# Routing by tiles, gathers and scatters that leave out empty places, results stored by token

## The reference

```python
def hier_moe(h, w_rg, w_re, w_g, w_u, w_d):
    T = h.shape[0]
    lg = (h @ w_rg).astype(jnp.float32)                 # 4 groups
    grp = jnp.argmax(lg, axis=-1)
    p_grp = jnp.take_along_axis(jax.nn.softmax(lg, axis=-1), grp[:, None], axis=-1)
    le = (h @ w_re).astype(jnp.float32).reshape(T, N_GROUPS, EXPERTS_PER_GROUP)
    le = jnp.take_along_axis(le, grp[:, None, None], axis=1)[:, 0]
    top_v, top_i = lax.top_k(le, TOP_K)                 # 2 experts of the group
    gates = p_grp * jax.nn.softmax(top_v, axis=-1)
    eid = (grp[:, None] * EXPERTS_PER_GROUP + top_i).astype(jnp.int32)
    return expert_dispatch(h, eid, gates.astype(h.dtype), w_g, w_u, w_d)
...
    # expert_dispatch, for each expert e and its tokens x:
    #   (silu(x @ w_g[e]) * (x @ w_u[e])) @ w_d[e], times the gate, summed by token
...
        x = x + mod[:, 5] * hier_moe(f_l, *moe_par).reshape(B, L, D)
```

## Time and profile before

| | |
|---|---|
| median of three runs | 2268.76 us |
| the profiled execution's own time | 2265.61 us |
| its span in the trace | 2263.5 us |
| PE busy | 1902.4 us (84%) |
| DVE busy | 814.9 us (36%) |
| ACT busy | 519.8 us (23%) |
| POOL busy | 82.5 us (4%) |
| moved by DMA | 376.37 MB |

### The profile page before, as it was taken

One profiled execution on the slowest core, in us unless ns is written; L12 is line 12 of the kernel. 1 busy time (PEld: TensorE's weight loads), 2 busy tenths in 40 slices (PEclk: granted clock), 3 DMA queues, 4 the chain that ended last, 5 costly groups with the idle time before them and its releaser, 6 DMA issues.

```text
span 2263.5 us, 29709 instructions
## 1 busy us (share of the span) xinstructions
PE 1902.4 (84%) x12822; PEld 1001.8 (44%) x12822; DVE 814.9 (36%) x1359; ACT 519.8 (23%) x957; POOL 82.5 (4%) x117
## 2 busy tenths in 40 slices
PE   5998569998998789978889889999974977777773
PEld 2443114643444555546666666664443332333231
DVE  2031533354645726434444544435335100000002
ACT  3001444321114512153233233113000000000001
POOL 0000000000000000020000000000000000000002
PEclk8999677599998899988899889999985999999997
DMA  8222343035111031031211111216415999999996
GB/s 338 75 74 75 112 159 139 27 137 218 59 37 38 0 135 47 0 127 43 67 49 54 62 43 49 90 35 270 159 64 224 416 428 426 426 427 426 428 427 242
DMA packets 49618, 376.37 MB, mean 166 GB/s; under 512 B 6033, under 2 KB 6177, under 8 KB 30795
## 3 DMA queue, kind: packets, MB, share of 16 engines
q1 hardware_dynamic: 36571, 317.85, 35.1%
q0 software_dynamic: 10032, 46.08, 5.6%
q10 hardware_dynamic: 2880, 10.49, 1.1%
HBM read 347.08 MB, written 31.51 MB: 167 GB/s over the span
## 4 chain that ended last, share of the span: by engine, by line
PE 40%; DMA 11%; DVE 8%; issue 2%; ACT 2%; POOL 0%; SPq 0%; DVEq 0%; ACTq 0%; POOLq 0%
PE psum L202 39%; DMA arena<-in_w 10%; DVE arena L149 4%; ACT arena L199 2%; DVE arena L159 1%; PE psum L205 1%; DVE arena L179 1%; DVE arena L167 1%; DVE arena L154 1%; DMA arena<-in_tok 0%; DVE arena L183 0%; DVE arena L187 0%; DVE arena L163 0%; DMA arena<-yd,arena 0%; DVE arena L175 0%
## 5 line engine op out<-in xcount | busy, mean ns | idle before, releaser
L202 PE MATMUL psum<-arena 64*64 64x32 f32 (+9 forms) x12174 | 1813.3, 372 | 303.0 <-ACT arena L199 104.2
L202 PEld LDWEIGHTS psum<-arena 64*64 64x64 f32 (+4 forms) x12174 | 922.5, 157 | 1135.3 <-issue 905.4
L199 ACT ACTIVATE arena<-psum 128x512 f32<-128x512 f32 (+6 forms) x389 | 206.5, 531 | 1195.9 <-PE psum L202 1083.2
L149 DVE TENSOR_TENSOR arena<-arena,psum 128x512 f32<-128x512 f32 (+1 forms) x136 | 75.5, 555 | 647.0 <-ACT arena L199 403.3
L199 ACT ACTIVATE arena<-arena 128x512 f32<-128x512 f32 (+10 forms) x242 | 135.4, 559 | 344.0 <-DVE arena L149 137.5
L149 DVE TENSOR_TENSOR arena<-arena 128x512 f32<-128x512 f32 (+11 forms) x312 | 195.4, 626 | 35.8 <-DMA arena<-in_norm_post 8.9
L149 DVE TENSOR_TENSOR arena<-psum,arena 128x256 f32<-128x256 f32 (+2 forms) x114 | 58.1, 509 | 253.8 <-PE psum L202 249.9
L159 DVE SCALAR_TENSOR_TENSOR arena<-arena 128x512 f32<-128x512 f32 (+5 forms) x138 | 111.4, 807 | 67.1 <-ACT arena L199 62.5
L205 PE MATMUL psum<-arena 128*128 128x128 f32 x648 | 108.3, 309 | 25.8 <-DVE arena L159 18.4
L205 PEld LDWEIGHTS psum<-arena 128*128 128x128 f32 x648 | 81.3, 157 | 93.3 <-issue 53.1
L199 ACT ACTIVATE arena<-psum,arena 128x128 f32<-128x128 f32 (+3 forms) x157 | 82.6, 526 | 173.0 <-PE psum L202 132.8
(11 more groups left out here) (46 smaller groups left out, 111.4 us busy)
## 6 DMA issues: line engine op xcount, KB each, us to landing
arena<-in_w SPq DMA_DIRECT2D x133, 2048.0 KB, 29.0
arena<-in_w SPq DMA_DIRECT2D x48, 256.0 KB, 3.0
yd<-arena ACTq DMA_DIRECT2D x16, 512.0 KB, 10.4
arena<-kd POOLq DMA_DIRECT2D x28, 256.0 KB, 3.9
gd<-arena SPq DMA_DIRECT2D x24, 256.0 KB, 3.1
arena<-gd SPq DMA_DIRECT2D x24, 256.0 KB, 8.4
yd<-in_zeros SPq DMA_DIRECT2D x1, 4096.0 KB, 18.6
arena<-in_w POOLq DMA_DIRECT2D x2, 2048.0 KB, 9.4
```

The source lines that it names most:

```text
L149: return self.ends(self.e.tensor_tensor(out, a, b, op))
L199: return self.ends(self.e.activation(out, a, func, **kw))
L202: return self.ends(self.e.matmul(out, lhs, rhs, start=start, stop=stop))
```

## The change

It does five things.

1. `gather` and `scatter` take `bounds_check=1023`, so a place whose index is over 1023 is left out. `IDX` now holds `NOBODY` = 2000 at empty places. POOL first fills the two `XG` buffers with zeros.
2. The result of a block no longer goes to `yd` by place from ACT, but is scattered by POOL to row `512 * j + token`, `j` being the first or second choice. For this `fd` is stored twice (rows 0 to 511 and 512 to 1023), so that one index serves for both. These stores move from ACT to POOL.
3. The tail reads `yd` in 8 plain loads of 128 rows from SP.
4. Ranks, places and the `slots` product are made tile by tile, woven between the output products; the order on PE, DVE and ACT changes with it, and ACT copies the turned tile ahead of the next tile's sum of squares.
5. What only the further blocks need (`EID`, their places and their `slots2` product) moves into the first 12 expert blocks, and the clearing of part of `yd` with zeros is gone.

```diff
     def gather(self, out, src, idx, signal):
-        self.e.indirect_dma_start(out, None, src, bass.IndirectOffsetOnAxis(ap=idx, axis=0)).then_inc(*signal)
+        self.e.indirect_dma_start(out, None, src, bass.IndirectOffsetOnAxis(ap=idx, axis=0), bounds_check=2 * S - 1, oob_is_err=False).then_inc(*signal)
...
     def scatter(self, dst, idx, src, signal):
-        self.e.indirect_dma_start(dst, bass.IndirectOffsetOnAxis(ap=idx, axis=0), src, None).then_inc(*signal)
+        self.e.indirect_dma_start(dst, bass.IndirectOffsetOnAxis(ap=idx, axis=0), src, None, bounds_check=2 * S - 1, oob_is_err=False).then_inc(*signal)
...
-    fd = internal("fd", (S, D))
-    yd = internal("yd", (128 * NB, D))
-    ydv = yd.rearrange("(r b) d -> r b d", b=NB)
+    fd = internal("fd", (2 * S, D))
+    yd = internal("yd", (2 * S, D))
+    ydv = yd.rearrange("(j t p) d -> j t p d", j=2, p=128)
...
-    fdv = fd.rearrange("(t p) d -> p t d", p=128)
+    fdv = fd.rearrange("(j t p) d -> j p t d", j=2, p=128)
...
+
...
+            def rank(i):
+                T.wait_ge(V["in", i], *ps.take(RANK, "rank", i))
+                T.mm(ps["rank", i][:, 0:32], C["tri"], IN[:, i, :], True, False)
+                T.mm(ps["rank", i][:, 0:32], ones, SUM[:, i, :], False, True).then_inc("rank", i)
+
+            def slots(i):
+                for j in range(2):
+                    T.wait_ge(V["slot", i, j])
+                    T.mm(ps["slots"][:, 0:NP], at_row(i, j), in_pair(i, j), (i, j) == (0, 0), (i, j) == (3, 1))
...
             for i in range(5):
                 if i < 4:
...
+                    out(i, 0)
+                if i > 1:
+                    rank(i - 2)
                 if i:
                     T.wait_ge(V["h3", i - 1])
...
+                    turn8("f4", i - 1, ht3[i - 1], SIX)
+                if i < 4:
+                    out(i, 1)
+                if i > 1:
+                    slots(i - 2)
+                if i:
+                    logits(i - 1)
+            rank(3)
+            slots(3)
             T.then_inc("slots")
+            T.wait_ge(*ps.take(RANK, "cnt"))
+            T.mm(ps["cnt"][:, 0:32], ones, SUM[:, 4, :], True, True).then_inc("cnt")
...
             for i in range(5):
+                if i:
+                    turn8_act("f4", i - 1, HT, i - 1)
                 if i < 4:
...
-                    A.wait_ge(V["h3", i])
-                    A.dma(fdv[:, i, :], ht3[i], d_fd.up(i))
-                if i:
-                    turn8_act("f4", i - 1, HT, i - 1)
...
+        def route_gpsimd():
+            G.wait_ge(T["ow", 0, 0], V["mg", 2, 7])
+            for b in XG:
+                G.zero(b)
+            G.mark("xg")
+            for i in range(4):
+                G.wait_ge(V["h3", i])
+                for j in range(2):
+                    G.dma(fdv[j, :, i, :], ht3[i], d_fd.up(j, i))
...
+                V.tt(SUM[:, i + 1, :], SUM[:, i, :], IN[:, i, :], ALU.add).then_inc("in", i)
+                V.ts(H64[:, i, :], EF[:, i, :], NP - 0.5, 64.0, ALU.is_ge, ALU.mult)
+                V.stt(COL[:, i, :], H64[:, i, :], -NP / 64.0, EF[:, i, :], ALU.mult, ALU.add)
+                for j in range(2):
+                    V.ts(in_pair(i, j), C["iota32"][:, 0:NP], COL[:, i, j:j + 1], TOKF[:, j, i:i + 1], ALU.is_equal, ALU.mult)
+
+            def place(i):
+
+                V.wait_ge(T["rank", i])
+                b, prod = ps["rank", i][:, 0:32], DM.rearrange("p (a j) e -> p a j e", a=2)[:, i % 2]
+                V.tt(prod, E12[:, i], bm(b, 2), ALU.mult)
+                V.red(R12[:, i, :].unsqueeze(2), prod, ALU.add)
+                V.ts(Q12[:, i, :], R12[:, i, :], 63.5, 1000.0, ALU.is_ge, ALU.mult)
+                V.tt(Q12[:, i, :], Q12[:, i, :], H64[:, i, :], ALU.add)
+                V.tt(P12[:, i, :], Q12[:, i, :], R12[:, i, :], ALU.add)
+                for j in range(2):
+                    V.ts(at_row(i, j), C["iota128"], P12[:, i, j:j + 1], None, ALU.is_equal).then_inc("slot", i, j)
+                V.cp(RK[:, i, :], b)
+                ps.free(V.last(), "rank", i)
 
...
+                    out(i, 0)
+                if i > 1:
+                    place(i - 2)
+                if i:
+                    turn8_dve("f4", i - 1, HT, i - 1)
+                if i < 4:
+                    out(i, 1)
                     V.then_inc("x2", i)
+                if i:
...
                 if i:
-                    route(i - 1)
-            V.then_inc("in")
...
+                    expert(i - 1)
+            place(3)
             V.wait_ge(T["slots"])
-            V.cp(IDX, ps["slots"][:, 0:NB]).then_inc("idx")
+            V.ts(IDX[:, 0:NP], ps["slots"][:, 0:NP], float(NOBODY), None, ALU.add).then_inc("idx")
             ps.free(V.last(), "slots")
-            V.cp(iovn, OVi[:, 31:32])
-            for j in range(2 * NO):
...
-            V.cp(iov, EID).then_inc("iov")
             V.ts(pg.unsqueeze(2), GM[:, :, 0:1], -1.0, None, ALU.mult)
...
+            V.wait_ge(T["cnt"])
+            V.cp(cnt, ps["cnt"][:, 0:32])
+            ps.free(V.last(), "cnt")
             V.mark("end5")
...
+        def over_slots_vector():
...
+            V.cp(iovn, OVi[:, 31:32])
+            for j in range(2 * NO):
+                V.ts(o1, OVi, j + 0.5, None, ALU.is_le)
+                V.red(EID[:, j:j + 1], o1, ALU.add)
+                if j % 4 == 3:
+                    yield
...
+            yield
+            V.wait_ge(T["slots2"])
+            V.ts(IDX[:, NP:NB], ps["slots2"][:, 0:NO], float(NOBODY), None, ALU.add)
...
         def experts_gpsimd():
-            G.wait_ge(V["idx"], d_fd[3])
-            for p in range(NP):
...
+            G.wait_ge(V["idx"], d_fd[1, 3], G["xg"])
+            for p in range(NP + 3):
+                if p < NP:
+                    if p > 1:
+                        G.wait_ge(T["tn", p - 2, 1])
+                    G.gather(XG[p % 2], fd, IDX[:, p:p + 1], d_xg[p % 2].up("xg", p))
+                if p > 2:
+                    G.wait_ge(A["yo", p - 3])
+                    G.scatter(yd, IDX[:, p - 3:p - 2], YO[(p - 3) % 2], d_yo[(p - 3) % 2].up("yo", p - 3))
+                if p == NP - 1:
+                    G.wait_ge(T["slots2"])
                     G.dma(rowC, mods2[0, 5120:6144].partition_broadcast(128), d_rc.up("rowC"))
...
+                over_slots(p)
...
+                if p:
+                    next(over_slots, None)
...
-                    A.wait_ge(A.last())
-                    A.dma(ydv[:, first + p - 1, :], YO[(p - 1) % 2], yo[(p - 1) % 2].up("yo", p - 1))
+                    A.mark("yo", p - 1)
...
         def tail_gpsimd():
-            tG.wait_ge(*end6(), d_y0["y0"])
-            for i in range(4):
-                for j in range(2):
-                    tG.gather(y12[i][j], yd, DI[:, i, j:j + 1], d_y12[i].up(j))
             for i in (0, 2):
...
         def tail_sync():
+            Y.wait_ge(*end6())
+            for i in range(4):
+                for j in range(2):
+                    Y.dma(y12[i][j], ydv[j, i], d_y12[i].up(j))
             for i in range(4):
                 Y.wait_ge(tV["x3", i] if i % 2 else tG["x3", i])
```

More of the change, by code:

```diff
@@ L27 @@
 WOVEN = 14
-SMALL = 1972
+SMALL = 1864
+NOBODY = 2000
 COL_SPEC = [
@@ L2116, in route_tensor, with out, logits @@
         def route_tensor():
-            T.wait_ge(V["mg", 2, 7])
+            def out(i, hf):
+                T.wait_ge(W.landed(43 + hf), *ps.take(SIX, "ow", i, hf))
+                for k in range(8):
+                    T.mm(ps["ow", i, hf], MG[:, k, c4(i)], wk(43 + hf)[:, k, :], k == 0, k == 7)
+                T.then_inc("ow", i, hf)
+                if i == 3:
+                    T.mark("w", 43 + hf)
+            def logits(i):
+                T.wait_ge(A["f4", i, 0], V["f4", i, 1], d_rt["wr"], *ps.take(SIX, "rt", i))
+                for k in range(8):
+                    T.mm(ps["rt", i][:, 0:36], HT[:, k, c4(i)], WRT[:, k, :], k == 0, k == 7)
+                T.then_inc("rt", i)
@@ new lines, in rank @@
+            def rank(i):
[6 more added lines that the diff above has]
+                    T.mm(ps["slots"][:, 0:NP], at_row(i, j), in_pair(i, j), (i, j) == (0, 0), (i, j) == (3, 1))
+            T.wait_ge(V["mg", 2, 7], *ps.take(SLOT, "slots"))
@@ L2162, in route_scalar, with out, group @@
             A.mark("end5")
+        def route_gpsimd():
[7 more added lines that the diff above has]
+                    G.dma(fdv[j, :, i, :], ht3[i], d_fd.up(j, i))
         def route_vector():
             ss = small
-            def route(i):
-                turn8_dve("f4", i, HT, i)
+            def out(i, hf):
+                xs = X[:, i, hf * 512:(hf + 1) * 512]
+                V.wait_ge(T["ow", i, hf])
+                V.tt(tt_[hf], ps["ow", i, hf], rowA[:, hf * 512:(hf + 1) * 512], ALU.mult)
+                ps.free(V.last(), "ow", i, hf)
+                V.wait_ge(d_xb["x"])
+                V.tt(xs, xs, tt_[hf], ALU.add)
+            def group(i):
                 V.wait_ge(T["rt", i])
```

(19 more changed lines are left out.)

171 lines of the change are left out of this document (83 added, 88 removed).

## The result

The changed kernel takes 2228.24 us (2227.04 to 2229.0, 4 runs) and the kernel before 2268.62 (2266.03 to 2268.77, 4 runs, three of them those of the table ahead of the prediction): ratio 0.9824, interval 0.9807 to 0.9841, faster by 40.4 us. The forecast was 2225.3, 43.5 less. The profiled execution took 2227.04 with a span of 2225.2, which is 38.3 under the span of before. They fall 5.2 us short of the forecast's 43.5, where the medians fall 3.1 short: the profiled execution of before was 3.0 under its median, and that of after 1.2.

The account below looks back on a forecast made before the run. Expert blocks were held bound by DMA, mostly weights, their start by routing; gains of 18.9 + 12.8 + 1.3 + 9.0 + 1.5 = 43.5 us took the median from 2268.76 to 2225.3, range 2212 to 2239.

Parts of the forecast that it names:

- likeliest case: Whole kernel: the forecast itself, its own terms leaving it at 2220 to 2231 us; chance 51%.
- Routing's tiles: From the end of `ow(1,1)` to that of `ow(3,1)`: 54.3 us become 35.4 without PE's pauses, gain 18.9 us.
- Routing's end: From `ow(3,1)` to the table: 37.7 us become 24.9, including 1.1 for hand-overs, gain 12.8 us.
- Table to block 0: From the table to block 0's first product: 12.2 us become 10.9 with a gather of 8.0, gain 1.3 us.
- EID: Ahead of block 0: moving it frees DVE when the turned tile comes, which takes out 2.8 us.
- Rows left out: Expert blocks' gathers and scatters: skipping empty places gains 9.0 us, taken between 0 and 18.1.
- third possibility: Expert blocks: DMA engines have fixed places and the fullest sets the end, gaining less than the mean, down to 0.
- rows shared evenly: Expert blocks: the heaviest DMA engine gains as much as the mean, 18.1 us for 9.0, giving 2216; chance 17%.
- empty places cost like full ones: Expert blocks: a descriptor is still made and moved for each, gain 0 for 9.0, giving 2234; chance 20%.
- slower rival: Expert blocks: transfers with rows left out run on fewer DMA engines; 2270.6 us with filled rows on four; chance 4%.
- Tail: After ACT's last copy: scatter loses 2.6 us, plain reads give 3 to 4 back; gain 1.5, between -2 and 4.
- The new order waits: Routing's tiles: `rank(i)` waits for DVE, PE pauses and a tile takes 22 us for 17.2, giving 2238; chance 8%.

Follow-up runs that it names:

- e7: The kernel before, with only ACT's copy of the turned tile moved ahead of the next tile's sum of squares and store: 2263.81 us, ratio 0.9991.
- e3: The changed kernel with empty places moved as full rows, reading a row of zeros and writing an unused row: 2236.98 us, ratio 0.9865 to the kernel before.
- e2: The changed kernel with an expert's first eight tokens in rows 0 to 3 and 32 to 35: 2235.61 us, ratio 0.9861 to the kernel before.
- e4: The changed kernel with the last two of eight weight loads held until block 0's gather landed: 2217.87 us, ratio 0.9790 to the kernel before.
- e5: The changed kernel with EID's 32 DVE operations back between index table and gates: 2227.27 us, ratio 0.9815 to the kernel before.
- e9: The changed kernel with two weight loads held for the first gather and EID back ahead of the gates: 2225.22 us, ratio 0.9813 to the kernel before.
- e10: The changed kernel run again unaltered, as base for its neighbours: 2226.62 us, ratio 0.9821 to the kernel before; first expert product to last 32 products 470.0 us.
- e1: The changed kernel with an expert's places dealt round, its first eight tokens in rows 0, 4, 8 to 28: 2222.35 us, ratio 0.9804 to the kernel before.

## Why the prediction was right, and where it was off

The result lies 2.9 us above the forecast and inside the likeliest case's own range, 2220 to 2231. By the two profiles the gain is 5.2 under the forecast: 1.9 of that is the later start, which no step foresaw and which lies within scatter. By its steps:

- **Routing's tiles: right.** 18.8 for 18.9, PE full at 1.00 as foretold. But the cause was half told. The prediction named ACT's copy alone; e7 shows that DVE's stood as far behind and that freeing one alone brings nothing that can be told. The sum came out since the change moves both.
- **Routing's end: 14.8 for 12.8.** Counted from the end of `ow(3,1)`, `rank(2)` was forecast at 8.5 us and came at 8.3, the last logits at 12.5 and 12.3, `rank(3)` at 19.4 and 19.1, the table at 23.8 and 22.9. The 1.1 us for hand-overs on top was wrong: durations read from the timeline held them already.
- **Table to block 0: the failed step.** It reads "With under half of the rows of block 0 filled I take 8.0, between the two." The gather took 10.6, and POOL issued it 0.9 after the table, which the sum left out: 2.6 and 0.9 account for the 3.4 us between +1.3 and -2.1. (Before, POOL issued it 0.3 after the table; why it is 0.9 now isn't shown.) Fewer rows hardly shorten a gather that lies behind weight loads. It took 10.6 with them left out and 11.2 with all moved (e3), and 11.4 with as many left out but on the fewest engines (e2). The load decides: 5.3 with two loads held (e4). The loss of 2.1 lies 0.4 outside the bound of -1.7, which lacked POOL's issue too.
- **`EID`**, which "takes 2.8 out": true of before, where DVE was late, but worth nothing beside a gather of 10.6 us (e5), and 4.2 where the gather is early (e9). The two terms weren't independent: a slower gather hides what the move gains.
- **Rows left out: 8.3 for 9.0.** The mechanism was the third possibility, named and half chosen. But 9.0 was the middle between 0 and 18.1 and followed from no row, so its hitting is luck: with the places of e2 the same mechanism gives about 1. The estimate by the rule of the Trainium skill ("DMA: Bandwidth & Descriptors", The descriptor swizzle) did work it out, 8.8, and agrees. By e10's 470.0 the weights gained 9.7, and PE's clock in the last groups took 1.4 back. The rivals *rows shared evenly* and *empty places cost like full ones* are both out, the one by e1 and e2, the other by e3. Of the slower rival nothing was seen: e2 puts the filled rows on as few engines as the placing allows and costs no more than before.
- **Tail: 0.3 for 1.5**, inside its bounds. Three lengths of the two traces take it apart. From the end of ACT's last copy to the issue of the first read it is 4.8 us (2193.92 to 2198.70) for 3.8 before (2231.88 to 2235.69), so the scatter lost 1.0 and not 2.6. From that issue to ACT's first operation it is 5.3 for 6.6 before: 1.3 back, not 3 to 4, since the plain reads landed 5.2 us after their issue instead of 3 to 4. From there to the end it is 21.2 us in both. DVE was busy 16.3 us for 15.8, and all of it is one operation beside POOL's addition, first before and then after:

```profile
2246.15 1.99 POOL L149 TENSOR_TENSOR arena<-arena 128x1024 f32<-128x1024 f32 x1 [0.53 <-DVE arena L149]
2246.71 2.51 DVE L159 SCALAR_TENSOR_TENSOR arena<-arena 128x1024 f32<-128x1024 f32 x1 [0.65 <-ACT arena L199]
```

```profile
2207.84 1.99 POOL L150 TENSOR_TENSOR arena<-arena 128x1024 f32<-128x1024 f32 x1 [12.17 <-DVE arena L150]
2207.90 3.02 DVE L160 SCALAR_TENSOR_TENSOR arena<-arena 128x1024 f32<-128x1024 f32 x1
```

The same operation takes 1.28 us with POOL idle (at 2205.20). It lay beside POOL's for 1.4 us before and lies beside it for 1.9 now; the 0.5 us longer stand in place of a wait of 0.65 for ACT, so they cost nothing.
- **The new order waits**: it doesn't, PE's idle time in the tiles is at most 0.21 us.

Of the signs that the prediction named against itself, the gather came near, 10.6 us where it had set 11, and PE and not the weights paced one group of products, the last but one.

## What to carry to other kernels

Leaving rows out of a transfer helps by what the fullest DMA engine is spared, not by the share left out: count the filled rows for each engine's partitions, and if they are uneven, deal them round by the order of the places. When a change moves a latency-bound transfer into a stretch full of large loads, price it by a transfer under load, whatever its size (here 10.6 us and not the 5.5 of a quiet queue), and ask whether one or two loads may wait for it. An edit that takes work away beside a wait is worth what the wait doesn't cover, so the two must be summed together.

## What was not expected of the hardware

A left-out place still counts as a packet (4032 with and without), yet costs little. Queue q0 held 19.8 us for 7.57 MB. By bytes alone, at the 36.3 us for 14.59 MB of before, it would be 18.8, which leaves about 1 us for all left-out places of the stretch together, with 0.2 of uncertainty from the rounding of the 4.3% alone.

The gathers inside the stream land later than before, 15.2 us after issue (14.7 to 15.6 in the other runs that leave rows out) for 11.0. The rows left out aren't the reason: e3 moves all of them, and its gathers land after 16.8 us. One thing that all of these runs share and the kernel before lacks is that scatters stand in POOL's queue too. No run took the scatters out of it, so it is not shown that they are the cause. PE waits for none of these gathers.
